# The delta rule's block elimination in other pieces, first retention states on ScalarE, decay exponentials earlier

## The chip, the cores and the metric

One core of a Trainium2 chip runs the whole program in one launch. Its engines each work through a queue of their own, in order: TensorE (PE, matrix products into PSUM), VectorE (DVE), ScalarE (ACT), GpSimd (POOL) and SyncE (SP, which issues DMAs). They wait for each other with semaphores only. The metric is device time in microseconds, the median of several runs.

## The reference

Two network blocks follow each other on 256 tokens of width 1024, in fp32. The first has dilated attention, a gated linear recurrence and two convolutional feed-forward parts. The change lies in the mixer of the second block, which works on 256 context tokens and 256 latent tokens: one projection gives queries, keys and values for four heads of a gated delta rule and four heads of retention, each run forward and backward.

```python
p = (h @ w_in)                         # qkv_a, z, ab, rq, rk, rv, rg
q, k, v = short_conv(qkv_a)            # 5 taps, silu
# gated delta rule, by chunks; G = cumsum of the log decay
decay = exp(G_i - G_j) for i >= j
A = strictly lower part of (beta k k^T * decay)
sol = (A + I)^-1 [beta v, beta k exp(G)]
v_new = u - w S;  o = q_dec S + (q k^T * decay) v_new;  S = g_last S + k_dec^T v_new
o_gdn = rms_norm(o_f + o_b) * silu(z)
# retention, by chunks
o = (q k^T * decay) v + xi (q R);  R = gamma^C R + (k zeta)^T v
o_ret = head_group_norm(r_f + r_b) * silu(rg)
y = concat(o_gdn, o_ret) @ w_out
```

## The kernel before, in words

Tokens are cut in four tiles of 128 (two of context, two latent). Each scan runs over tiles, `TILE_OF` gives the order for the two directions (`DIRS`), and `STEPS` is 4; only steps 2 and 3, the latent tiles, give outputs. fp32 weight products are split: a unit is an eighth of a 2 MB weight chunk or a 128-column strip of it; ACT writes its high part (`high_parts`, L340), DVE subtracts and writes the low part (`low_parts`, L344), and PE multiplies the parts. There are three slots for units (`NPARTS`), so the high part of unit n waits until PE has used unit n-3. The chunks of `w_in` come in the order K, RV, V, RK, Q, Z, RQ, RG, four units each, counted from `u0`: k is 0 to 3, rv 4 to 7, v 8 to 11, rk 12 to 15, q 16 to 19, z 20 to 23, rq 24 to 27, rg 28 to 31. `low_parts(dve, u0 + n)` does all units up to n-1.

The order on every engine is written out by hand, line after line, and is what the change edits.

PE (L2395 to L2511): k, rv, then the v units. Ahead of v's last unit it waits for `EX`, since that unit's bank holds the sums of log decays until ACT has taken their exponential (`EX`, L1373). Then come rk units with log-decay differences and key products between them (`differences`, `key_products`), transposes of v, the units of q, z, rq and rg, transposes of rq and rk, and the retention steps (L2489 to L2511).

ACT (L1365 to L1436): in the loop over v's convolutions i = 4 to 7 it takes a tap (`conv_taps`), a tanh (`conv_tanh`), at i = 5 four copies of turned keys and then `EX`; after the loop the exponentials of the differences (`decay`), then `store_matrix`, which writes the matrices A to DRAM. SP reads their 32x32 diagonal blocks back (L952 to L957) as `blocks`, one block for each partition, and ACT turns the half that belongs to the backward direction (L1395). At the end ACT waits for `inverses`, stores both halves of the inverted blocks to DRAM (L1429, L1432) and loads half of the rows back (L1435); SP loads the other half (L963).

DVE (L1885 to L2043): between the low parts it rotates rk and rq (`rotated`), convolves q (`conv`, `conv_out`), scales z and rg (`gated`) and inverts all blocks at once by elimination (`eliminate`, L1901): for column j it multiplies a column by a row (L1906) and subtracts (L1908), two instructions of up to 240 elements, each waiting for the one before. The columns 1 to 30 stand in six pieces behind low parts. Then the retention steps: update the states (`update_state`, with a plain copy at step 0), mask and multiply the scores (`rPm`), add up outputs (`output_part`). At step 3 DVE expands the inverse rows (`expand`, L1989), from which the delta rule's chain begins: PE's `turn_inverse` (L2537) is its first step.

Of the kernel before, what the change touches and what calls it, by code (L numbers as in the profile page):

```python
# [13 lines left out]
P = 128  # L14
# [101 lines left out]
def build_program(nc, A, out):  # L116
    ctx = ExitStack()
    with ctx:
# [795 lines left out]
        def _(sp):  # L914
# [42 lines left out]
                    sp.dma_start((turned_blocks if d else blocks)[at:at + HB, :, :], source).then_inc(S_("blocks_in"), 16)  # L957
            for i in range(begin_gather, begin_rows):
                load(i)
            sp.wait_ge(S_("inverses_out"), 32)  # L960
            w_rg.done(sp)
            for b in range(NB):
                sp.dma_start(inverse_rows[b * BLK:(b + 1) * BLK, 1, :, :],  # L963
                             block_inverses.ap()[1, b, :, :, :].rearrange("n i j -> i n j")).then_inc(S_("inverse_rows_in"), 16)
            resume = -(-begin_rows // NS)
            for i in range(begin_rows, resume * NS):
                load(i)
# [120 lines left out]
        def _(act):  # L1088
# [276 lines left out]
            for i in range(4, 8):  # L1365
                high_parts(act, u0 + 8 + i)
                conv_taps(i)
                conv_tanh(i)
                if i == 5:
                    for t in range(TT2):  # L1370
                        turned("knT", t)
                    act.wait_ge(S_("sums"), 1)
                    nc_a.activation(EX[:, :, :, :].rearrange("p a b c -> p (a b c)"), ps[:, SUMS_BANK, 0:320], ACT.Exp).then_inc(S_("EX"), 1)  # L1373
            for n in range(4):
                decay(n)
            high_parts(act, u0 + 16)
            for n in (0, 1):
# [46 lines left out]
            for t in LATENT:  # L1424
                turned("rqT", t)

            act.wait_ge(S_("inverses"), 1)
            stored = block_inverses.ap().rearrange("d b n i j -> d (b n) (i j)")
            act.dma_start(stored[0], blocks_flat[0:P // 2, :]).then_inc(S_("inverses_out"), 16)  # L1429
            nc_a.activation(turned_flat[P // 2:P, :], blocks_flat[P // 2:P, ::-1], ACT.Copy).then_inc(S_("blocks_turned"), 1)  # L1430
            act.wait_ge(S_("blocks_turned"), 2)
            act.dma_start(stored[1], turned_flat[P // 2:P, :]).then_inc(S_("inverses_out"), 16)  # L1432
            act.wait_ge(S_("inverses_out"), 32)
            for b in range(NB):
                act.dma_start(inverse_rows[b * BLK:(b + 1) * BLK, 0, :, :],  # L1435
                              block_inverses.ap()[0, b, :, :, :].rearrange("n i j -> i n j")).then_inc(S_("inverse_rows_in"), 16)  # L1436
            def head_squares(kind, t):

                for h in range(H4):
# [106 lines left out]
        def _(dve):  # L1546
# [347 lines left out]
            rotated(w_rk, 0, rk[:, 0, :, :], 0)  # L1894
            low_parts(dve, u0 + 20)
            conv(8)
            rotated(w_rk, 1, rk[:, 1, :, :], 1)
            low_parts(dve, u0 + 21)
            conv_out(8)
            conv(9)  # L1900
            def eliminate(first, end):  # L1901

                for j in range(first, end):
# [7 lines left out]
                    else:  # L1911
                        last.then_inc(S_("inverses"), 1)

            dve.wait_ge(S_("blocks_in"), 16 * 2 * NB)
            dve.wait_ge(S_("blocks_turned"), 1)
            link(v.memset(blocks_flat[:, 0:BLK * BLK:BLK + 1], -1.0))
            eliminate(1, 7)
            low_parts(dve, u0 + 22)
            conv_out(9)
            conv(10)  # L1920
            eliminate(7, 10)
            low_parts(dve, u0 + 23)
            conv_out(10)
            conv(11)
            eliminate(10, 13)
            low_parts(dve, u0 + 24)
            conv_out(11)
            rotated(w_rk, 2, rk[:, 2, :, :], 2)
            low_parts(dve, u0 + 25)
            rotated(w_rk, 3, rk[:, 3, :, :], 3)  # L1930
            eliminate(13, 18)
            low_parts(dve, u0 + 27)
            for i in range(TT):
                gated(w_z, i, zt, TT2)
            eliminate(18, 22)
            low_parts(dve, u0 + 28)
            eliminate(22, BLK - 1)
            for t in LATENT:
                normalized("qn", t)
            low_parts(dve, u0 + 29)  # L1940
            low_parts(dve, u0 + 30)
            low_parts(dve, u0 + 31)
            w_rq.done(dve)
            rotated(w_rq, 0, rq[:, 0, :, :], 0)
            low_parts(dve, u0 + 32)
            rotated(w_rq, 1, rq[:, 1, :, :], TT2 + TT + 1)
            dve.wait_ge(S_("tok_vector"), TT2 + 2 * TT)

            def bc(a):
# [65 lines left out]

            for i in range(TT):
                gated(w_rg, i, rgt, TT2 + TT)
            for d in DIRS:
                dve.wait_ge(S_("decay"), 2 * TT2 + d + 1)
                link(v.tensor_tensor(rET[d], rET[d], bh(cst[:, C_GE if d else C_LE, :]), ALU.mult))  # L2020

            for step in range(STEPS):
                if step >= 2:
                    for d in DIRS:
                        if step > 2:
                            dve.wait_ge(S_("ro"), later(step - 1, d))
                        dve.wait_ge(S_("rqk"), later(step, d))
                        v.tensor_tensor(rPm[d], B4(4 * d), rET[d], ALU.mult).then_inc(S_("rPm"), 1)
                if step < 3:
                    for d in DIRS:  # L2030
                        dve.wait_ge(S_("rdS"), nth(step, d))
                        update_state(rSt[d], 1, step, d, 4 * d + 3, S_("rstate"))
# [155 lines left out]
        def _(pe):  # L2188
# [300 lines left out]
            for step in range(STEPS):  # L2489
                if step >= 2:  # L2490
                    for d in DIRS:
                        t = TILE_OF[d][step]
                        if step > 2:
                            pe.wait_ge(S_("rPm"), later(step - 1, d))
                        heads(4 * d, tile(rkT, t), tile(rqT, t - TT)).then_inc(S_("rqk"), 1)
                    for d in DIRS:
                        t = TILE_OF[d][step]
                        pe.wait_ge(S_("rstate"), nth(step - 1, d))
                        if step > 2:
                            pe.wait_ge(S_("o_out"), later(step - 1, d))  # L2500
                        heads(4 * d + 1, tile(rqT, t - TT), rSt[d])
                if step < 3:
                    for d in DIRS:
                        pe.wait_ge(S_("rkdec"), nth(step, d))
                        if step:
                            pe.wait_ge(S_("rstate"), nth(step - 1, d))
# [276 lines left out]
```

## Time and profile before

| | us |
|---|---|
| median of 3 runs | 1341.31 (1339.39 to 1343.09) |
| span of the profiled execution | 1335.4 |
| PE busy | 1264.9 (95%) |
| DVE busy | 913.2 (68%) |
| ACT busy | 695.0 (52%) |
| POOL busy | 77.0 (6%) |
| PE in the chain that ended last | 78% of the span |

The page gives the span of the profiled execution and no other time of it; the times of the runs are taken apart from it. Engines can be busy at the same time, so the shares don't add up. The mixer of the second block takes the span from about 836 to 1103 us; what the diff touches lies between 896 and 1038 us.

### The profile page before, as it was taken

To read this page: it belongs to the slowest core of one execution; us is meant where nothing else is said; L and a number is where in the kernel's file an instruction comes from. 1 tells how busy PE (TensorE), PEld (TensorE's weight loads), DVE (VectorE), ACT (ScalarE), POOL (GpSimd) and SP (SyncE) were. 2 spreads that over 40 slices of the span, in tenths; PEclk is the share of its full clock that TensorE was granted. 3 is DMA by queue.
4 is the path that set the end of the run, shared out by engine and by line. 5 is a ranking of instruction groups with operands and counts; after the bars stand their busy time and mean duration, and the time that the engine had idled before them with its cause. 6 is when DMAs were issued, how large, how long until landed. Compare 5 with 4: busy or idle time off the path is not lost.

```text
span 1335.4 us, 19244 instructions
## 1 busy us (share of the span) xinstructions
PE 1264.9 (95%) x7760; PEld 1080.7 (81%) x7760; DVE 913.2 (68%) x1429; ACT 695.0 (52%) x1132; POOL 77.0 (6%) x126
## 2 busy tenths in 40 slices
PE   7999999999999999999999999999979889899997
PEld 5899988877888887987888876786758876788885
DVE  4464553447888857687888876755796886766665
ACT  5454544446666645766666755334332444455553
POOL 1000000001000001001000001022011301000000
PEclk9999999999999999999999999999989899899999
DMA  9844335556555557257555557212533006555551
GB/s 336 327 172 145 127 126 190 189 186 241 192 189 192 186 200 265 93 190 291 189 190 189 189 189 266 72 64 103 165 124 101 2 1 212 200 189 191 191 200 48
DMA packets 31718, 230.74 MB, mean 173 GB/s; under 512 B 11000, under 2 KB 14704, under 8 KB 18704
## 3 DMA queue, kind: packets, MB, share of 16 engines
q1 hardware_dynamic: 25568, 218.14, 45.3%
q10 hardware_dynamic: 5056, 7.73, 1.6%
q0 software_dynamic: 1008, 3.67, 0.7%
q8 instruction: 61, 1.00, 0.3%
q14 instruction: 25, 0.20, 0.0%
HBM read 225.82 MB, written 3.71 MB: 172 GB/s over the span
## 4 chain that ended last, share of the span: by engine, by line
PE 78%; DVE 12%; ACT 6%; issue 2%; DMA 1%; POOL 1%; SPq 0%; DVEq 0%; POOLq 0%; ACTq 0%
PE ps L436 18%; PE ps L620 16%; PE ps L499 10%; PE ps L440 9%; PE ps L208 8%; PE ps L488 5%; PE ps L587 4%; DVE parts L344 3%; PE ps L559 3%; PE ps L531 2%; ACT parts L340 2%; DMA ring<-in_W 1%; DVE arena L1655 1%; DVE row L1908 1%; DVE arena L1906 1%
## 5 line engine op out<-in xcount | busy, mean ns | idle before, releaser
L344 DVE TENSOR_TENSOR parts<-ring,parts 128x1024 fp32r<-128x1024 f32 x354 | 431.4, 1224 | 278.5 <-ACT parts L340 201.0
L340 ACT ACTIVATE parts<-ring 128x1024 fp32r<-128x1024 f32 x354 | 372.7, 1057 | 296.6 <-PE ps L440 102.6
L436 PE MATMUL ps<-hall,parts 128*128 128x512 f32 x1120 | 395.1, 398 | 5.5 <-DVE hall L293 3.7
L440 PE MATMUL ps<-hall,parts 128*128 128x256 f32 x1120 | 313.8, 280 | 0.0
L620 PE MATMUL ps<-parts 128*128 128x512 f32 x1128 | 262.0, 391 | 8.6 <-DVE parts L375 8.3
L436 PEld LDWEIGHTS ps<-hall,parts 128*128 128x128 f32 x1120 | 211.1, 188 | 58.4 <-issue 3.3
L620 PEld LDWEIGHTS ps<-parts 128*128 128x128 f32 x1128 | 210.0, 188 | 57.9 <-DVE parts L375 12.6
L440 PEld LDWEIGHTS ps<-hall,parts 128*128 128x128 f32 x1120 | 212.3, 190 | 0.0
L499 PE MATMUL ps<-hall,parts 128*128 128x256 f32 x1152 | 140.7, 284 | 0.0
L499 PEld LDWEIGHTS ps<-hall,parts 128*128 128x128 f32 x1152 | 139.0, 192 | 0.6 <-DVE parts L344 0.5
L208 PE MATMUL ps<-arena 128*128 128x128 f32 (+4 forms) x934 | 111.7, 285 | 16.4 <-DMA arena<-in_onehot 6.5
L208 PEld LDWEIGHTS ps<-arena 128*128 128x128 f32 (+3 forms) x934 | 101.7, 182 | 24.7 <-issue 6.6
L587 PE MATMUL ps<-parts,hall 128*128 128x512 f32 x336 | 85.9, 414 | 8.8 <-DVE parts L344 8.8
L1655 DVE SCALAR_TENSOR_TENSOR arena<-arena,par 128x255 f32<-128x255 f32 (+1 forms) x192 | 80.0, 479 | 18.5 <-ACT arena L1178 17.6
L587 PEld LDWEIGHTS ps<-parts,hall 128*128 128x128 f32 x336 | 66.1, 199 | 25.6 <-DVE parts L344 10.8
L488 PE MATMUL ps<-parts,hall 128*128 128x512 f32 x288 | 69.2, 400 | 1.4 <-DVE hall L297 0.9
L312 POOL TENSOR_SCALAR smallp<-small 128x1 f32<-128x1 f32 x24 | 10.8, 451 | 983.2 <-ACT arena L673 605.7
L488 PEld LDWEIGHTS ps<-parts,hall 128*128 128x128 f32 x288 | 55.2, 193 | 14.6 <-DVE parts L344 3.1
L559 PE MATMUL ps<-hall,parts 128*128 128x512 f32 (+1 forms) x288 | 59.8, 365 | 4.7 <-issue 2.8
L559 PEld LDWEIGHTS ps<-hall,parts 128*128 128x128 f32 x288 | 47.9, 193 | 15.6 <-issue 5.1
L531 PE MATMUL ps<-hall,parts 128*128 128x256 f32 x384 | 48.8, 290 | 1.8 <-DVE hall L297 1.8
L531 PEld LDWEIGHTS ps<-hall,parts 128*128 128x128 f32 x384 | 48.0, 197 | 2.2 <-DVE gates L1576 2.0
(213 smaller groups left out, 1066.0 us busy)
## 6 DMA issues: line engine op xcount, KB each, us to landing
ring<-in_W SPq DMA_DIRECT2D x100, 2048.0 KB, 8.3
arena<-distance_tables SPq DMA_DIRECT2D x8, 384.0 KB, 8.0
gains<-in_gains POOLq DMA_DIRECT2D x5, 512.0 KB, 8.1
ring<-in_W SPq DMA_DIRECT2D x4, 512.0 KB, 9.1
arena<-in_gate_w ACTq DMA_DIRECT2D x1, 2048.0 KB, 10.6
matrices<-arena ACTq DMA_DIRECT2D x8, 256.0 KB, 2.3
x<-in_x SPq DMA_DIRECT2D x2, 512.0 KB, 5.3
gates<-in_ada_gate_b POOLq DMA_DIRECT2D x2, 512.0 KB, 6.3
```

The lines of the kernel that those rows point to most:

```text
L208: return nc.tensor.matmul(o, l, r, start=start, stop=stop)
L340: return nc.scalar.activation(unit_weights(n, 0, weights), weights, ACT.Copy)
L344: return nc.vector.tensor_tensor(unit_weights(n, 1, weights), weights, unit_weights(n, 0, weights), ALU.subtract)
L436: last = nc.tensor.matmul(ps[:, b, :].rearrange("p (a b) -> p a b", a=2), w[:, 0, :], hparts[:, :, k, :], start=k == 0, stop=False)
L440: last = nc.tensor.matmul(ps[:, b, 0:S], w[:, 1, :], hparts[:, 0, k, :], start=False, stop=k == KT - 1)
L488: last = nc.tensor.matmul(ps[:, banks[t], :], hparts[:, x_part, k, t * P:(t + 1) * P], parts[:, u % NPARTS, w_part, w0:w0 + 512], start=k ...
L499: last = nc.tensor.matmul(ps[:, banks[n // 2], (n % 2) * S:(n % 2 + 1) * S], parts[:, u % NPARTS, w_part, k * P:(k + 1) * P], hparts[:, x_ ...
L531: last = nc.tensor.matmul(ps[:, 4 + 2 * (i % 2) + n // 2, (n % 2) * S:(n % 2 + 1) * S], parts[:, u % NPARTS, w_part, k * P:(k + 1) * P], h ...
L559: last = nc.tensor.matmul(o, parts[:, u % NPARTS, w_part, k * P:(k + 1) * P], h, start=k == 0 and x_part == 1, stop=k == KT - 1 and w_part ...
L587: last = nc.tensor.matmul(ps[:, b, :], hall[:, t // TT, x_part, k, t % TT * P:(t % TT + 1) * P], parts[:, u % NPARTS, w_part, w0:w0 + 512] ...
L620: last = nc.tensor.matmul(ps[:, 2 * t + half, :], parts[:, n % NPARTS, x_part, D + t * P:D + (t + 1) * P], parts[:, n % NPARTS, w_part, w0 ...
L1655: last = v.scalar_tensor_tensor(dst, src, pcol("ffn_conv_w", (layer * 3 + tap) * 48 + ft), dst, ALU.mult, ALU.add)
```

## The change: what it does

On ACT `EX` moves ahead of the tanh at i = 5, and the first two decay exponentials ahead of the tanh at i = 7. The copy that turns the backward blocks goes from i = 9 to i = 10, and the high part of unit 23 goes ahead of tanh 11. After the turned queries ACT copies the first retention states (`first_rstate`), and once the inverses are there it turns the backward half and stores it. It then scales the between-tile part of retention's step 2 out of PSUM into the output (`retained`), to which DVE only adds the other part.

On DVE the rotations 0 and 1 of rk come first, then the low parts 19 to 23 with the convolutions of q between them; the elimination starts behind the low part of unit 25 and goes in seven pieces of 3, 2, 2, 3, 2, 4 and 14 columns. The last piece stands behind the gating of rg, directly ahead of the retention steps. The mask of `rET` moves to step 2.

On SP the forward half of the inverses is stored, and all eight loads of rows are issued there, where before ACT issued both stores and four of the loads. PE's waits in the retention follow the new counts.

```diff
 SP
-            sp.wait_ge(S_("inverses_out"), 32)
+            sp.wait_ge(S_("inverses"), 1)
+            sp.dma_start(block_inverses...[0], blocks_flat[0:P // 2, :]).then_inc(S_("inverse_out0"), 16)
             w_rg.done(sp)
-            for b in range(NB):
-                sp.dma_start(inverse_rows[..., 1, :, :], block_inverses.ap()[1, b]...)
+            for d in DIRS:
+                sp.wait_ge(S_(f"inverse_out{d}"), 16)
+                for b in range(NB):
+                    sp.dma_start(inverse_rows[..., d, :, :], block_inverses.ap()[d, b]...)
 ACT
                 conv_taps(i)
+                if i == 5:
+                    act.wait_ge(S_("sums"), 1)
+                    nc_a.activation(EX..., ps[:, SUMS_BANK, 0:320], ACT.Exp).then_inc(S_("EX"), 1)
+                if i == 7:
+                    for n in range(2):
+                        decay(n)
                 conv_tanh(i)
...
-            for n in range(4):
+            for n in range(2, 4):
                 decay(n)
...
-                if i == 9:
+                if i == 10:
                     act.wait_ge(S_("blocks_in"), 16 * 2 * NB)
...
+            high_parts(act, u0 + 24)
             conv_tanh(11)
...
+            for d in DIRS:
+                act.wait_ge(S_("rdS"), nth(0, d))
+                nc_a.activation(rSt[d], B4(4 * d + 3), ACT.Copy).then_inc(S_("first_rstate"), 1)
             act.wait_ge(S_("inverses"), 1)
-            act.dma_start(stored[0], ...)
             nc_a.activation(turned_flat[P // 2:P, :], blocks_flat[P // 2:P, ::-1], ACT.Copy)
-            act.dma_start(stored[1], ...)
-            act.wait_ge(S_("inverses_out"), 32)
-            for b in range(NB): act.dma_start(inverse_rows[..., 0, :, :], ...)
+            act.dma_start(block_inverses...[1], turned_flat[P // 2:P, :]).then_inc(S_("inverse_out1"), 16)
+            for d in DIRS:
+                act.wait_ge(S_("rdS"), nth(2, d))
+                for h in range(H4):
+                    last = nc_a.activation(y2[1][:, t - TT, h, :], ps[:, 4 * d + 1, h * P:(h + 1) * P],
+                                           ACT.Copy, scale=EX[...])
+                last.then_inc(S_("retained"), 1)
 DVE, new order
+            rotated rk 0, rk 1; low_parts(u0 + 20); conv(8)
+            for i in range(8, 12):
+                low_parts(dve, u0 + 13 + i)
+                conv_out(i)
+                if i < 11:
+                    conv(i + 1)
+            rotated rk 2; low_parts(u0 + 25); rotated rk 3; low_parts(u0 + 26)
             dve.wait_ge(S_("blocks_in"), ...); dve.wait_ge(S_("blocks_turned"), 1); memset
+            eliminate(1, 4);   gated z;       low_parts(u0 + 27)
+            eliminate(4, 6);   low_parts(u0 + 28)
+            eliminate(6, 8);   normalized qn; low_parts(u0 + 29)
+            eliminate(8, 11);  low_parts(u0 + 30); rotated rq 0; low_parts(u0 + 31)
+            eliminate(11, 13); low_parts(u0 + 32); rotated rq 1
+            eliminate(13, 17); gated rg
+            eliminate(17, BLK - 1)
 DVE, retention
+                if step == 2 and kind == 1:
+                    dve.wait_ge(S_("retained"), d + 1)
+                    v.tensor_tensor(o_, o_, B4(inner), ALU.add).then_inc(S_("o_out"), 1)
+                    return
...
-                if step < 3:
+                if step in (1, 2):
 PE, retention
-                        pe.wait_ge(S_("rstate"), nth(step - 1, d))
+                        pe.wait_ge(S_("rstate"), nth(step - 2, d))
                         if step > 2:
                             pe.wait_ge(S_("o_out"), later(step - 1, d))
+                            pe.wait_ge(S_("retained"), d + 1)
...
+                        if step == 1:
+                            pe.wait_ge(S_("first_rstate"), d + 1)
```

## Rows read from the trace of the kernel before

**Rows 1.** Page, busy us of each engine (share of span) and instructions.
```profile
PE 1264.9 (95%) x7760; PEld 1080.7 (81%) x7760; DVE 913.2 (68%) x1429; ACT 695.0 (52%) x1132; POOL 77.0 (6%) x126
```
**Rows 2.** Waits of PE, 902 to 1045: us in total, times, longest.
```profile
PE ps L587 <- DVE parts L344: 8.8, 4, 3.2
PE ps L2355 <- DVE arena L1839: 3.1, 1, 3.1
```
**Rows 3.** Chain that ended last, 880 to 1060: start us, us, what.
```profile
896.90 5.54 PE ps L559 x24
902.45 2.85 issue
905.29 7.28 PE ps L559 x24
...
944.93 1.75 PE ps L2355 x16
...
1004.82 10.91 PE ps L587 x48
```
**Rows 4.** Timeline of ACT: start us, us, line, instructions [idle before <- releaser].
```profile
902.83 2.04 ACT L1331 ACTIVATE arena<-ps 128x512 f32<-128x512 f32 x4
904.73 0.46 ACT L1373 ACTIVATE arena<-ps 128x320 f32<-128x320 f32 x1
...
1040.84 1.11 ACT L1462 ACTIVATE arena<-ps 32x128 f32<-32x128 f32 x4 [0.85 <-PE ps L208]
```
**Rows 5.** Stages: us, busy PE, PEld, DVE, ACT, POOL, clock, DMA share, GB/s.
```profile
946.06:1017.65 71.59, 59.62 (x298) 49.66 (x297) 60.18 (x125) 26.73 (x52) 5.56 (x6) 0.88 0.36 115
...
964.32:970.04 5.72, 5.49 (x13) 3.80 (x13) 5.41 (x13) 0.89 (x2) 0.00 (x0) 0.50 0.00 0
...
1000.14:1004.57 4.43, 4.43 (x24) 4.25 (x25) 4.43 (x5) 1.79 (x3) 0.00 (x0) 0.61 0.29 122
...
1018.30:1019.83 1.53, 0.04 (x2) 0.00 (x1) 0.86 (x2) 1.50 (x5) 0.00 (x0) 1.00 0.94 403
...
1022.16:1037.40 15.24, 14.74 (x129) 14.55 (x129) 12.40 (x34) 0.00 (x0) 2.98 (x3) 1.00 0.29 51
```
**Rows 6.** Timeline of PE: z's first unit and the first turn_inverse.
```profile
958.18 2.91 PE L587 MATMUL ps<-parts,hall 128*128 128x512 f32 x12
...
1037.40 1.04 PE L2537 MATMUL ps<-cst,arena 128*128 128x128 f32 x8
```
**Rows 7.** Waits of DVE, 946 to 1037.4: us in total, times, longest.
```profile
DVE parts L344 <- ACT parts L340: 8.4, 3, 4.2
DVE arena L1832 <- ACT arena L1406: 4.6, 1, 4.6
```
**Rows 8.** Stretches, DVE busy of L1906 alone (first three), of L1908 (last).
```profile
946.06:1017.65 71.59, 9.92 (x30) 0.88 0.36 115
959.39:963.04 3.65, 1.56 (x6) 1.00 0.81 346
984.80:1000.00 15.20, 4.55 (x14) 0.89 0.30 101
...
984.80:1000.00 15.20, 4.57 (x14) 0.89 0.30 101
```
**Rows 9.** Timeline of SP's queue: four loads of inverse rows.
```profile
1023.73 2.56 SPq L963 DMA_DIRECT2D arena<-block_inverses x4
```
**Rows 10.** DMA issues, 1015 to 1036: KB each, median us to landing.
```profile
block_inverses<-row ACTq DMA_DIRECT2D x1, 256.0 KB, 4.1
...
arena<-block_inverses SPq DMA_DIRECT2D x4, 64.0 KB, 2.8
```
**Rows 11.** Timeline of DVE in the retention: mask, update of both directions, rPm.
```profile
1017.65 1.54 DVE L2020 TENSOR_TENSOR arena<-arena,cst 128x512 f32<-128x512 f32 x2
...
1023.36 2.16 DVE L1979 SCALAR_TENSOR_TENSOR arena<-arena,ps 128x128 f32<-128x128 f32 x8 [0.75 <-PE ps L208]
1025.43 1.40 DVE L2028 TENSOR_TENSOR arena<-ps,arena 128x512 f32<-128x512 f32 x2
```

More of the change, by code:

```diff
@@ L1367, in _ @@
                 conv_taps(i)
+                if i == 5:
+                    act.wait_ge(S_("sums"), 1)
+                    nc_a.activation(EX[:, :, :, :].rearrange("p a b c -> p (a b c)"), ps[:, SUMS_BANK, 0:320], ACT.Exp).then_inc(S_("EX"), 1)
+                if i == 7:
+                    for n in range(2):
+                        decay(n)
                 conv_tanh(i)
@@ L1371, in _ @@
                         turned("knT", t)
-                    act.wait_ge(S_("sums"), 1)
-                    nc_a.activation(EX[:, :, :, :].rearrange("p a b c -> p (a b c)"), ps[:, SUMS_BANK, 0:320], ACT.Exp).then_inc(S_("EX"), 1)
-            for n in range(4):
+            for n in range(2, 4):
                 decay(n)
@@ L1425, in _ @@
                 turned("rqT", t)
+            for d in DIRS:
+                act.wait_ge(S_("rdS"), nth(0, d))
+                nc_a.activation(rSt[d], B4(4 * d + 3), ACT.Copy).then_inc(S_("first_rstate"), 1)
             act.wait_ge(S_("inverses"), 1)
-            stored = block_inverses.ap().rearrange("d b n i j -> d (b n) (i j)")
-            act.dma_start(stored[0], blocks_flat[0:P // 2, :]).then_inc(S_("inverses_out"), 16)
             nc_a.activation(turned_flat[P // 2:P, :], blocks_flat[P // 2:P, ::-1], ACT.Copy).then_inc(S_("blocks_turned"), 1)
             act.wait_ge(S_("blocks_turned"), 2)
-            act.dma_start(stored[1], turned_flat[P // 2:P, :]).then_inc(S_("inverses_out"), 16)
-            act.wait_ge(S_("inverses_out"), 32)
-            for b in range(NB):
-                act.dma_start(inverse_rows[b * BLK:(b + 1) * BLK, 0, :, :],
-                              block_inverses.ap()[0, b, :, :, :].rearrange("n i j -> i n j")).then_inc(S_("inverse_rows_in"), 16)
+            act.dma_start(block_inverses.ap().rearrange("d b n i j -> d (b n) (i j)")[1],
+                          turned_flat[P // 2:P, :]).then_inc(S_("inverse_out1"), 16)
+            for d in DIRS:
+                t = TILE_OF[d][2]
+                act.wait_ge(S_("rdS"), nth(2, d))
+                for h in range(H4):
+                    last = nc_a.activation(y2[1][:, t - TT, h, :], ps[:, 4 * d + 1, h * P:(h + 1) * P], ACT.Copy,
+                                           scale=EX[:, C_GE if d else C_LE, t, 8 + 4 * d + h:9 + 4 * d + h])
+                last.then_inc(S_("retained"), 1)
             def head_squares(kind, t):
@@ L1893, in _ @@
             w_rk.done(dve)
[L1894 to L1900, printed above, removed]
             def eliminate(first, end):
@@ L1912, in eliminate @@
                         last.then_inc(S_("inverses"), 1)
+            rotated(w_rk, 0, rk[:, 0, :, :], 0)
+            rotated(w_rk, 1, rk[:, 1, :, :], 1)
+            low_parts(dve, u0 + 20)
+            conv(8)
+            for i in range(8, 12):
[3 more added lines that the diff above has]
+                    conv(i + 1)
+            rotated(w_rk, 2, rk[:, 2, :, :], 2)
+            low_parts(dve, u0 + 25)
+            rotated(w_rk, 3, rk[:, 3, :, :], 3)
+            low_parts(dve, u0 + 26)
             dve.wait_ge(S_("blocks_in"), 16 * 2 * NB)
@@ L1916, in _ @@
             link(v.memset(blocks_flat[:, 0:BLK * BLK:BLK + 1], -1.0))
[L1917 to L1932, printed above, removed]
+            eliminate(1, 4)
             for i in range(TT):
                 gated(w_z, i, zt, TT2)
-            eliminate(18, 22)
+            low_parts(dve, u0 + 27)
+            eliminate(4, 6)
             low_parts(dve, u0 + 28)
-            eliminate(22, BLK - 1)
+            eliminate(6, 8)
             for t in LATENT:
@@ L1940, in _ @@
             low_parts(dve, u0 + 29)
+            eliminate(8, 11)
             low_parts(dve, u0 + 30)
-            low_parts(dve, u0 + 31)
             w_rq.done(dve)
             rotated(w_rq, 0, rq[:, 0, :, :], 0)
+            low_parts(dve, u0 + 31)
+            eliminate(11, 13)
             low_parts(dve, u0 + 32)
             rotated(w_rq, 1, rq[:, 1, :, :], TT2 + TT + 1)
+            eliminate(13, 17)
             dve.wait_ge(S_("tok_vector"), TT2 + 2 * TT)
@@ L2017, in _ @@
                 gated(w_rg, i, rgt, TT2 + TT)
-            for d in DIRS:
-                dve.wait_ge(S_("decay"), 2 * TT2 + d + 1)
-                link(v.tensor_tensor(rET[d], rET[d], bh(cst[:, C_GE if d else C_LE, :]), ALU.mult))
+            eliminate(17, BLK - 1)
             for step in range(STEPS):
+                if step == 2:
+                    for d in DIRS:
+                        dve.wait_ge(S_("decay"), 2 * TT2 + d + 1)
+                        link(v.tensor_tensor(rET[d], rET[d], bh(cst[:, C_GE if d else C_LE, :]), ALU.mult))
                 if step >= 2:
@@ L2504, in _ @@
                         pe.wait_ge(S_("rkdec"), nth(step, d))
-                        if step:
-                            pe.wait_ge(S_("rstate"), nth(step - 1, d))
+                        if step == 1:
+                            pe.wait_ge(S_("first_rstate"), d + 1)
+                        elif step:
+                            pe.wait_ge(S_("rstate"), nth(step - 2, d))
                         heads(4 * d + 3, rkdec[d], rv[:, TILE_OF[d][step], :, :]).then_inc(S_("rdS"), 1)
```

7 lines of the change are left out of this document (5 added, 2 removed).

## The prediction, made before the changed kernel was run

> **What bounds the kernel now.** I read the page's busy shares first: TensorE (PE) works in 95% of the span [rows 1], so a gain can only come from the few stretches in which PE waits or runs at half clock. Next I read whom PE waited for between 902 and 1045 us, the stage that the diff touches [rows 2]: 8.8 us in four pieces for low parts that VectorE (DVE) writes, and 3.1 us for the scaled queries (L1839), again DVE. The chain of waits adds a third stop [rows 3]: a piece called "issue", 2.85 us from 902.45. The reader should see that it is no issue at all. PE's program waits there for `EX` ahead of the last v unit, and ScalarE's (ACT's) Exp that signals it runs from 904.73 to 905.19 [rows 4]; PE goes on at 905.29.
>
> Then the stage windows. From 958.18, where the z units begin [rows 6], to the end of rg at 1015.7 PE spends 57.5 us. The twelve units of z, rq and rg at the full-clock price (10.91 us for four, so 2.73 each [rows 3]) are 32.7; sixteen transposes and sixteen decay products between them, at retention's 14.74 us for 128 [rows 5], are about 3.7. So some 21 us are lost: 11.9 in the waits of rows 2, and the rest because PE falls to half clock after them. One z unit took 5.49 us at a granted clock of 0.50; a later stretch had 0.61 [rows 5].
>
> Why is DVE late? From 946.06 to 1017.65 it works almost without a break [rows 5]: its own waits there are 4.2 us for high parts (8.4, less the 4.2 that ends at 946.06) and 4.6 for the rg tanh [rows 7]. The elimination is 30 columns of two instructions, twice 9.9 us busy [rows 8] and about 1.9 of links, 21.8 together, and it stands in pieces in front of the low parts in DVE's one queue: 3.65 us of it ahead of the first z part that PE waits for [rows 8]. In the retention, from 1022.16 to 1037.40, PE is the bound: 14.74 us busy of 15.24 [rows 5].
>
> **The change part by part.** I follow one place: when does PE begin the first `turn_inverse`, at 1037.40 now [rows 6]? All behind it is a chain of small steps among PE, DVE and ACT and then two PE-bound projections; the diff touches none of it, so it moves along rigidly.
>
> *EX ahead of tanh 5.* The Exp needs the sums, ready by 897, and then comes behind tap 5, at about 899. PE reaches its wait at 902.45 and no longer stops: 2.85 us. The v unit behind it took 7.28 us for 24 matmuls against 5.54 for the unit before [rows 3]: 1.74 of half clock, gone too if no stop comes. What is late next: the first rk unit needs the knT copies, done at 904.87 [rows 4], and PE comes at 907.99, so nothing. Of the decay exps 0 and 1 now run ahead of tanh 7; PE wants their banks at about 916, ACT has them by 913.5. So the end of the rk units, 944.93 [rows 3], becomes 940.34, 4.59 earlier. If ACT's order still held PE, this term would be 0.
>
> *DVE's order.* The low part that opens the window of rows 5 starts 1.13 behind the rk units: 941.47. DVE's work from there to the end of both elimination and gated rg is what it is now, 71.59 us less 8.8 of waits, 62.8; only the order differs. Does it wait in the new order? I laid it against PE, instruction by instruction with the durations of the trace. z's four low parts end at 951, 954.5, 958 and 961.5; PE wants them at 953.6, 956.4, 959.1 and 961.8. The fourth rk tile is rotated at 967.0, PE wants it at 965.5: a stop of 1.5. The rq parts come at 965, 968.2, 972.2 and 974.6, wanted at 967, 969.7, 972.5 and 975.2; the rg parts come ahead too. In turn DVE finds each high part ready and waits only some 0.4 us for the rg tanh. PE ends rg near 992 in place of 1015.7, and DVE ends the elimination at 941.47 + 62.8 + 0.4 = 1004.7. PE's 23 us are not the gain: DVE is now the bound, and its last fourteen columns (4.55 + 4.57 busy [rows 8], 10.0 with links) stand in front of retention's second state.
>
> *The block gather* is on SP's queue behind the rq weights, which wait for the last rk unit, so it lands 4.6 earlier too, while ACT's copy of the blocks now comes one tap later. It costs nothing; landing late, it would hold ACT's taps and with them z's low parts, us for us.
>
> *Retention.* ACT's two copies of the first states replace DVE's. A copy of 512 columns is about 0.5 on ACT (four in 2.04 [rows 4]); they lie beside GpSimd's second decayed keys, for which PE waits anyway: nothing, at most 0.2. PE is through two state products and rqk at about 1003.2 and then waits for the state of step 1: 1004.7 plus one direction, half of 2.16 [rows 11], is 1005.8. Six groups of 16 matmuls are left to it; eight took 14.74 [rows 5], so 1.84 each and 11.1: 1016.9. DVE holds them up by 0.3, since 2.16 of update, 1.54 of mask and 1.40 of rPm [rows 11] come first: 1017.2. The `retained` pieces on ACT, 128 columns out of PSUM with a column factor, are not in this trace: between 0.13 each (a quarter of a copy) and 0.5 (a whole one). I take 0.28, the nearest row, four pieces of 128 columns in 1.11 [rows 4], so 1.1 for a direction. They start at the third state product, about 1009, and DVE comes for them at 1012: nothing, and 1 us at the upper end. DVE saves 1.1 us for each direction in step 2, inside PE's six groups: no gain at the end.
>
> *Inverses through DRAM.* SP now stores one half and issues all loads; ACT stores the other. From 1004.7: 4.1 us for the store [rows 10], eight loads on one queue at 2.56 for four [rows 9], so 5.1, and 2.8 to land [rows 10]: 1016.7, and DVE's `expand` needs them. With its 0.64 the transposes start at 1017.4. Now two queues share the loads and the rows arrive 7 us early; then the path is level with PE's. The new waits hold nothing else: behind SP's stands the next weight load, whose chunk is used near 1100; behind ACT's its own share of the retention.
>
> *Clock.* PE stops for some 2.5 us at 1003.2, as it waits for DVE's columns. After the stops of 2.85 and 3.2 us in this trace the next work took 1.74 and 2.76 longer [rows 3, 5]; a stop of 1.5 at 1018.30 cost nothing [rows 5]. I put 1.8 on the path, with ends 0 and 2.8: 1019.2.
>
> **Sum.** 1037.4 - 1019.2 = 18.2 us, so a span of 1335.4 - 18.2 = 1317.2. The page gives no time of the profiled execution beside its span; the median of the runs, 1341.31, is 5.9 above the span, and I carry that over: 1323.1, written as 1323.
>
> **Rivals.**
> *Half clock all through the retention.* For it: granted clock 0.50 from 964 to 970, where PE went at DVE's pace [rows 5]. Against it: in the retention now it is 1.00 in spite of a stop of 1.5 us just ahead [rows 5]. Six groups at twice 1.84 add 11.1 in place of 1.8: a gain of 8.9, 1332.4. The Trainium skill, page "TensorE: Matmul & The Clock Gate", section "What's actually happening", says that the chip halves PE's clock by how busy PE has lately been. By that rule this rival is the regular case wherever PE goes at DVE's pace, and the time would be 1332.4; the trace agrees in the stretches of rows 5 at 0.50 and 0.61, and cannot show it for the new retention.
>
> *The EX wait gives way to another.* PE stops at the knT copies, a difference or a key product instead, and the 4.59 come back: a gain of 13.6, 1327.7. For it: ACT and DVE are only 1 to 3 us ahead of PE there in my layout. Against it: rows 2 name no other engine that PE had to wait for there.
>
> *Slower: the backlog comes back behind the tail.* If z and rq are late because of all of DVE's other work (fourteen low parts, rotations, convolutions) and not of the columns, nothing is won ahead, and 10.0 us of columns follow gated rg: the elimination ends at 1027.7, the transposes start 12.7 + 1.8 later, at 1042.2, 4.8 later than now: 1346. It decides if gated rg ends after 1012.9 (now 1017.65). Against it: the part that PE waits for first has 3.65 us of columns directly in front of it [rows 8], more than the 3.2 that PE waits. That the pieces don't leave the low parts' path is the same case.
>
> **How the numbers follow.** Forecast, 1319 to 1327, 0.62; half clock all through 0.16; EX 0.10; better than 1319 0.04; slower 0.04; a mixture that ends within 4 us of now 0.04. Three thousandths, 4 us, is about what a measurement of this kernel can tell from no change. The time is 1323. The low end, 1317, lies 4 below the same sum without the clock's 1.8, since DVE's short rows may pack better than laid out; the high end, 1333, takes in the half clock. Faster 0.92, same 0.04, slower 0.04.
>
> **What would show it.** After the change: no "issue" piece at 902 in the chain; no wait of PE on L344 above 1 us between 950 and 1000, and a granted clock of 1.00 there; rg ended by 993 to 996; the last columns ended by 1004 to 1007 and PE waiting behind them for the update; `turn_inverse` near 1019. It is wrong if PE's waits on L344 in this stage still sum to 5 us, if DVE stands idle for several us ahead of the last columns, or if `expand` waits long for its rows.

## The result and the profile after

The changed kernel takes 1323.19 us (median of 4 runs, 1321.14 to 1326.27), the kernel before, run beside it, 1340.35 (median of 4, 1334.72 to 1343.09). The ratio is 0.9884 with an interval of 0.9862 to 0.9906: 17.2 us less. The profiled execution has a span of 1319.3 us, 16.1 below that of the kernel before; its own time was 1321.14. Of the runs of the kernel before that stand beside the experiments, one took 1572.18 us at a granted clock of 0.749 and is left out of the median given there.

Absolute times drift by more than 4 us between executions already ahead of the changed stage. So I compare stages from one mark, the piece of the chain with the sums of log decays (ten matmuls of L208; 895.84 before, 895.74 after), to the first `turn_inverse`. I call this the stage length: 141.56 us before, 126.18 after, 15.4 less.

The busy shares, which answer to [rows 1]:

```profile
PE 1256.0 (95%) x7760; PEld 1075.7 (82%) x7760; DVE 915.2 (69%) x1419; ACT 697.8 (53%) x1142; POOL 78.4 (6%) x126
```

PE is busy 8.9 us less with the same 7760 matmuls: that is half clock gone, not work (in the stage the granted clock rose from 0.93 to 0.97). The chain of waits from the mark on (start us, us, what) answers to [rows 3]:

```profile
895.74 1.06 PE ps L208 x10
896.80 10.99 PE ps L559 x48
907.78 2.72 PE ps L587 x12
...
929.23 10.93 PE ps L587 x48
940.18 1.07 ACT parts L340
...
991.53 1.26 DVE row L1917
992.82 1.14 DVE arena L1915
...
1009.67 12.42 PE ps L208 x96
```

The v units are one piece of 10.99 us, where before a stop of 2.85 and a slow unit of 7.28 stood. From 940 to 1009 the chain now runs through DVE: it is the bound of the stage. PE's waits from 896 to 1045 (us in total, times, longest), against [rows 2]:

```profile
PE ps L208 <- DVE arena L1994: 7.3, 1, 7.3
PE ps L208 <- ACT arena L1335: 1.9, 1, 1.9
PE ps L587 <- DVE arena L1844: 1.2, 1, 1.2
```

All waits on L344 are gone. One long one is new, for the state update (L1994) behind the last columns. The stretches (us, busy time of PE, PEld, DVE, ACT, POOL, clock, DMA share, GB/s) answer to [rows 5]:

```profile
958.00:996.00 38.00, 34.89 (x183) 29.42 (x182) 36.62 (x70) 17.92 (x39) 4.80 (x6) 1.00 0.47 168
941.27:1008.49 67.22, 57.55 (x350) 50.58 (x348) 64.49 (x125) 30.02 (x58) 9.25 (x10) 0.98 0.43 139
...
1009.67:1011.69 2.02, 2.02 (x9) 2.02 (x10) 1.99 (x6) 0.00 (x0) 0.00 (x0) 0.50 0.98 229
1011.69:1013.80 2.11, 2.11 (x17) 2.11 (x16) 1.57 (x3) 0.00 (x0) 0.00 (x0) 0.76 0.55 96
1013.80:1021.92 8.12, 8.12 (x75) 8.12 (x74) 7.36 (x17) 2.17 (x8) 0.00 (x0) 1.00 0.32 50
```

The granted clock is 1.00 from 958 to 996, where it fell to 0.50 and 0.61 before. After the wait of 7.28 us it is low for only 4.1 us. But DVE's stretch, from the first low part to the end of the elimination, is 67.2 us long, where the prediction had 63.2 (62.8 of work, 0.4 of a wait). The surplus stands in a few lines of DVE's timeline (start us, us, line, operation, shapes):

```profile
991.53 1.25 DVE L1917 TENSOR_TENSOR row<-row,arena 128x240 f32<-128x240 f32 x1
992.82 1.13 DVE L1915 TENSOR_TENSOR arena<-row 128x240 f32<-128x240 f32 x1
993.98 0.41 DVE L1917 TENSOR_TENSOR row<-row,arena 128x240 f32<-128x240 f32 x1
...
997.38 1.11 DVE L1915 TENSOR_TENSOR arena<-row 128x228 f32<-128x228 f32 x1
998.52 1.12 DVE L1917 TENSOR_TENSOR row<-row,arena 128x228 f32<-128x228 f32 x1
999.67 1.14 DVE L1915 TENSOR_TENSOR arena<-row 128x220 f32<-128x220 f32 x1
1000.85 1.12 DVE L1917 TENSOR_TENSOR row<-row,arena 128x220 f32<-128x220 f32 x1
1002.00 0.38 DVE L1915 TENSOR_TENSOR arena<-row 128x210 f32<-128x210 f32 x1
```

Six instructions of one kind take 1.11 to 1.25 us, their neighbours of the same shape 0.38 to 0.41. GpSimd's timeline shows what ran beside them: retention's decayed keys, in these two stretches and nowhere else in the stage:

```profile
991.48 2.21 POOL L1039 TENSOR_TENSOR arena<-arena 128x512 f32<-128x512 f32 x2 [20.97 <-PE ps L587]
997.02 4.70 POOL L1039 TENSOR_TENSOR arena<-arena 128x512 f32<-128x512 f32 x4 [3.34 <-PE ps L208]
```

In the kernel before, the same keys began at 1015.89, and the last column had ended at 999.5:

```profile
1015.89 2.04 POOL L1035 TENSOR_TENSOR arena<-arena 128x512 f32<-128x512 f32 x2 [28.06 <-PE ps L587]
```

The two never met there. The change brings them together from both sides: PE is through with rg earlier, so the keys start earlier, and the columns end later.

### The profile page after: what moved, and what is told of

Read it like the earlier page. It is cut to its first block, busy times and chain, and to the rows that moved or that the text cites. A ratio compares the mean times of both kernels' runs of the same rounds, so it can differ in the third digit from the quotient of the medians.

```text
span 1319.3 us, 19248 instructions
## 1 busy us (share of the span) xinstructions
PE 1256.0 (95%) x7760; PEld 1075.7 (82%) x7760; DVE 915.2 (69%) x1419; ACT 697.8 (53%) x1142; POOL 78.4 (6%) x126
## 4 chain that ended last, share of the span: by engine, by line
PE 78%; DVE 13%; ACT 6%; issue 2%; DMA 1%; POOL 1%; SPq 0%; DVEq 0%; POOLq 0%; ACTq 0%
PE ps L436 19%; PE ps L620 16%; PE ps L499 10%; PE ps L440 10%; PE ps L208 8%; PE ps L488 5%; DVE parts L344 4%; PE ps L587 3%; PE ps L559 3%; ACT parts L340 2%; PE ps L531 2%; DMA ring<-in_W 1%; DVE row L1917 1%; DVE arena L1915 1%; DVE arena L1671 1%
## 5 line engine op out<-in xcount | busy, mean ns | idle before, releaser
L344 DVE TENSOR_TENSOR parts<-ring,parts 128x1024 fp32r<-128x1024 f32 x354 | 433.0, 1227 | 272.4 <-ACT parts L340 193.2
L436 PEld LDWEIGHTS ps<-hall,parts 128*128 128x128 f32 x1120 | 211.4, 189 | 59.1 <-issue 2.8
L440 PEld LDWEIGHTS ps<-hall,parts 128*128 128x128 f32 x1120 | 212.0, 189 | 0.0
L499 PEld LDWEIGHTS ps<-hall,parts 128*128 128x128 f32 x1152 | 139.0, 192 | 0.6 <-DVE parts L344 0.5
L208 PE MATMUL ps<-arena 128*128 128x128 f32 (+4 forms) x934 | 113.8, 288 | 23.4 <-DVE arena L1994 7.3
L208 PEld LDWEIGHTS ps<-arena 128*128 128x128 f32 (+3 forms) x934 | 103.5, 185 | 31.9 <-DVE arena L1994 7.5
L587 PE MATMUL ps<-parts,hall 128*128 128x512 f32 x336 | 79.0, 393 | 1.2 <-DVE arena L1844 1.2
L587 PEld LDWEIGHTS ps<-parts,hall 128*128 128x128 f32 x336 | 62.6, 188 | 14.8 <-DVE arena L1844 1.5
L488 PE MATMUL ps<-parts,hall 128*128 128x512 f32 x288 | 68.3, 397 | 1.4 <-DVE hall L297 0.9
L488 PEld LDWEIGHTS ps<-parts,hall 128*128 128x128 f32 x288 | 54.6, 191 | 14.3 <-DVE parts L344 3.0
L559 PEld LDWEIGHTS ps<-hall,parts 128*128 128x128 f32 x288 | 48.3, 193 | 10.5 <-issue 1.8
L1182 ACT ACTIVATE arena<-arena,par 128x256 f32<-128x256 f32 x96 | 49.6, 588 | 0.2 <-DVE arena L419 0.2
```

The source lines that it names most:

```text
L208: return nc.tensor.matmul(o, l, r, start=start, stop=stop)
L344: return nc.vector.tensor_tensor(unit_weights(n, 1, weights), weights, unit_weights(n, 0, weights), ALU.subtract)
L436: last = nc.tensor.matmul(ps[:, b, :].rearrange("p (a b) -> p a b", a=2), w[:, 0, :], hparts[:, :, k, :], start=k == 0, stop=False)
L440: last = nc.tensor.matmul(ps[:, b, 0:S], w[:, 1, :], hparts[:, 0, k, :], start=False, stop=k == KT - 1)
L488: last = nc.tensor.matmul(ps[:, banks[t], :], hparts[:, x_part, k, t * P:(t + 1) * P], parts[:, u % NPARTS, w_part, w0:w0 + 512], start=k ...
L499: last = nc.tensor.matmul(ps[:, banks[n // 2], (n % 2) * S:(n % 2 + 1) * S], parts[:, u % NPARTS, w_part, k * P:(k + 1) * P], hparts[:, x_ ...
```

## The experiments

The theory going in: DVE's columns ahead of the low parts had stopped PE, `EX` was a stop of its own, and both are gone; DVE is now the bound, lengthened by GpSimd's keys. The first four ran together, with 1339.20 for the kernel before (median of 15), then the other four, with 1338.35 (median of 7).

**`EX` back in its old place, all else as changed.**

```diff
-                if i == 5:          # ahead of conv_tanh(i)
-                    act.wait_ge(S_("sums"), 1)
-                    nc_a.activation(EX..., ACT.Exp).then_inc(S_("EX"), 1)
                 conv_tanh(i)
                 if i == 5:
                     for t in range(TT2):
                         turned("knT", t)
+                    act.wait_ge(S_("sums"), 1)
+                    nc_a.activation(EX..., ACT.Exp).then_inc(S_("EX"), 1)
```

> The changed kernel with one edit undone: the exponential that signals EX stands again behind the four copies of turned keys, after the tanh of i = 5. Theory (each edit pays by its own stop): PE stops for 2.85 us ahead of the last v unit and does 24 matmuls at partly half clock, 7.3 in place of 5.5; the rk units end 4.6 us later, VectorE's long stretch of work starts 4.6 later, and all behind it moves with it: first turn_inverse 4.6 later than 1021.9, time 4.6 above the changed kernel (range 3.5 to 5.5). Rival (VectorE is the bound from before that place and absorbs the stop): turn_inverse and time move by less than 1.5 us.

Measured: 1328.32 us (1325.07 to 1330.24, 5 runs), ratio to the kernel before 0.9924 (0.9899 to 0.995). The stage is 129.86 us long, 3.7 more than in the changed kernel. Its chain:

```profile
896.98 5.54 PE ps L559 x24
902.53 2.87 issue
905.39 5.73 PE ps L559 x24
```

The stop is back at its full size. The unit behind it took 5.73 us, 0.2 over its neighbour, where it took 1.74 over in the kernel before. At the end of the rk units 3.2 of the 3.7 us are there already; the rest came behind them. So `EX` is a stop of its own, as the theory had it, and what varies is the half clock after it.

**Decayed keys on ScalarE instead of GpSimd.**

```diff
 POOL
-            for step in range(STEPS - 1):
-                for d in DIRS: ... decayed_keys(1, step, d, rkdec, rk, S_("rkdec"))
 ACT, around the first_rstate copies
+            def retention_keys(step, d):
+                for h in range(H4):
+                    last = nc_a.activation(rkdec[d][:, h, :], rk[:, t, h, :], ACT.Copy, scale=EX[...])
+                last.then_inc(S_("rkdec"), 1)
```

> The changed kernel with retention's decayed keys (three steps, two directions) on ScalarE, four scaled copies of 128 columns each, in place of GpSimd's six multiplications. In the changed kernel six instructions of the elimination took 1.11 to 1.25 us where their like took 0.39 to 0.42, all six beside those multiplications. Theory (VectorE and GpSimd slow each other while both read two tensors of SBUF): no elimination instruction above 0.45 us, the last column ends 4.4 us earlier (1004.1), PE's wait for the update shrinks from 7.3 to about 3, first turn_inverse at 1017 to 1018 and time 4 to 5 us below the changed kernel. Rival (the six long instructions are VectorE's own, for instance a wait or a PSUM or DMA collision at that time): they stay long, and the time is unchanged or up to 2 us worse, as ScalarE takes 1.1 us for a direction where GpSimd took 1.04.

Measured: 1317.91 us (1317.69 to 1318.33, 5 runs), ratio 0.9845 (0.982 to 0.9871); stage 120.42, 5.8 shorter than the changed kernel's. The groups of DVE's instructions in the two lines of the elimination (count, busy us, mean ns, idle before), first of the changed kernel, then of this one:

```profile
L1917 DVE TENSOR_TENSOR row<-row,arena 128x30 f32<-128x30 f32 (+14 forms) x30 | 12.3, 409 | 1.0
L1915 DVE TENSOR_TENSOR arena<-row 128x30 f32<-128x30 f32 (+14 forms) x30 | 12.1, 404 | 0.8
```

```profile
L1924 DVE TENSOR_TENSOR row<-row,arena 128x30 f32<-128x30 f32 (+14 forms) x30 | 10.0, 333 | 1.0
L1922 DVE TENSOR_TENSOR arena<-row 128x30 f32<-128x30 f32 (+14 forms) x30 | 9.9, 330 | 0.8
```

24.4 us fall to 19.9, what the kernel before spent on them, and the last column ends 4.5 us earlier after the mark. PE's timeline shows the rest:

```profile
999.25 3.64 PE L208 MATMUL ps<-arena 128*128 128x128 f32 x16 [2.72 <-ACT arena L1433]
...
1004.79 14.09 PE L208 MATMUL ps<-arena 128*128 128x128 f32 x120 [0.49 <-ACT arena L1433]
1018.71 1.04 PE L2566 MATMUL ps<-cst,arena 128*128 128x128 f32 x8
```

PE no longer stops for the update, only for ACT's keys: three waits, the longest 2.72 us. From the last column's end (1006.58) to `turn_inverse` it takes 12.1 us in place of 13.4, with the granted clock at 1.00 from 1004.79 on. So 4.5 of the 5.8 us are the columns' own, and 1.3 are won behind them, where PE neither stops nor runs at half clock. This is the lowest median measured, below both kernels.

**Columns back ahead of z's low parts.**

```diff
             for i in range(8, 12):
+                if i == 9: (waits for the blocks, memset)
+                if i > 8:
+                    eliminate(*{9: (1, 7), 10: (7, 10), 11: (10, 13)}[i])
                 low_parts(dve, u0 + 13 + i)
...
-            eliminate(1, 4)      and (4, 6), (6, 8), (8, 11), (11, 13) further down
```

> The changed kernel with the first twelve columns of the elimination moved back ahead of z's second, third and fourth low parts (6, 3 and 3 columns); the columns 13 to 30 stay where the change put them. VectorE does the same work in another order. Theory (columns ahead of low parts make PE stop, and VectorE then has to wait for PE): PE waits for low parts come back, three of 1.5 to 3 us, with granted clocks of 0.5 to 0.8 behind them; rg ends at about 1000 in place of 991, the elimination at about 1016 in place of 1008.5, time 8 us above the changed kernel (range 5 to 11). Rival (the backlog is all of VectorE's other work, the place of the columns is of no account): time within 2 us of the changed kernel.

Measured: 1330.75 us (1327.43 to 1333.9, 10 runs), ratio 0.9937 (0.9921 to 0.9953); stage 133.42, 7.2 longer than the changed kernel's. PE's waits and its fourth z unit:

```profile
PE ps L587 <- DVE parts L344: 7.3, 3, 2.9
PE ps L208 <- DVE arena L1992: 5.6, 1, 5.6
```

```profile
974.03 5.49 PE L587 MATMUL ps<-parts,hall 128*128 128x512 f32 x12 [2.90 <-DVE parts L344]
```

Twelve columns in the old place bring back the waits and a unit at half clock (5.49 us, the length it had in [rows 5]). DVE pays too: it waits 8.6 us longer for high parts, since PE frees their slots later. That is how the columns' place moves the end of the elimination, 7.3 us later after the mark, though the work is the same. What the theory said came, and the rival's 2 us did not, but for the clock: it fell behind the third stop alone (0.50), and was 1.00 in the units behind the other two. The 7.2 us are a net figure: the keys meet narrower columns here, and the two lines of the elimination take 22.9 us instead of 24.4.

**The kernel before with columns 1 to 29 left out.**

```diff
-                for j in range(first, end):
+                for j in range(max(first, BLK - 2), end):
```

> The kernel before with the elimination's columns 1 to 29 left out (column 30 stays, to signal), so the inverses are not computed; everything else in its order. Theory (the columns are what made z, rq and rg late): PE has no wait above 1 us for a low part between 950 and 1000, granted clock 1.00 there, rg ends near 997 in place of 1015.6, and the time falls by 18 to 20 us. Rival (VectorE's other work is enough to hold PE up): waits for low parts of 5 us or more stay, and the time falls by less than 8 us.

Measured, in one run: 1328.91 us, 10.3 below the kernel before; stage 126.53, 15.0 shorter (the profiled execution reached the mark 4.2 us later than that of the kernel before, so the two differ). Its waits of PE:

```profile
PE ps L559 <- issue: 2.9, 1, 2.9
PE ps L587 <- DVE parts L344: 2.3, 2, 1.9
PE ps L587 <- DVE arena L1828: 1.6, 1, 1.6
```

This lies between the theory's figure and the rival's. The columns are most of it, but 3.9 us of stops stay though 29 of the 30 columns are gone (the granted clock behind them is 1.00, as the theory had it). DVE's rotations and convolutions also stood ahead of low parts, and the reorder moves those as well; that they cause these stops was not tested by itself. The unit after the `EX` stop took 8.58 us here. By the stage length the changed kernel, with all its columns, is as quick as the old order without them, which still has the `EX` stop.

**Decayed keys on GpSimd with a factor for each partition, one tensor read in place of two.**

```diff
-                    decayed_keys(1, step, d, rkdec, rk, S_("rkdec"))
+                    for h in range(H4):
+                        last = nc.gpsimd.tensor_scalar(rkdec[d][:, h, :], rk[:, t, h, :], EX[...], None, ALU.mult)
+                    last.then_inc(S_("rkdec"), 1)
```

> The changed kernel with retention's decayed keys still on GpSimd, but as four multiplications of 128 columns by a column factor (one tensor of SBUF read, not two). With these keys off GpSimd no elimination instruction was above 0.41 us, so GpSimd is the other party; open is whether it matters what GpSimd reads. Theory (two two-tensor readers collide): no elimination instruction above 0.45, the last column 4.4 us earlier than in the changed kernel, counted from the sums of log decays (112.7 there), turn_inverse 3 to 5 earlier. Rival (any GpSimd multiplication beside VectorE's two-tensor instructions collides): elimination instructions of 1 us and more stay beside the keys, as many or more of them, as four instructions take GpSimd longer, and time is unchanged to 3 us worse.

Measured: 1319.05 us (1318.2 to 1323.76, 4 runs), ratio 0.9864 (0.9838 to 0.9889); stage 122.97, 3.2 shorter than the changed kernel's. DVE's two lines, and two of their instructions:

```profile
L1919 DVE TENSOR_TENSOR arena<-row 128x30 f32<-128x30 f32 (+14 forms) x30 | 11.2, 374 | 0.8
L1921 DVE TENSOR_TENSOR row<-row,arena 128x30 f32<-128x30 f32 (+14 forms) x30 | 11.2, 374 | 1.0
```

```profile
999.54 0.54 DVE L1921 TENSOR_TENSOR row<-row,arena 128x220 f32<-128x220 f32 x1
1000.12 0.54 DVE L1919 TENSOR_TENSOR arena<-row 128x210 f32<-128x210 f32 x1
```

GpSimd's 24 instructions of 128 elements took 636 ns each, 14.8 us in all, where six of 512 took 1122 ns each, 6.7 in all. The collision is not gone but has another form: DVE's instruction beside them lasts 0.54 us instead of 1.12, over about twice the time. So the last column ends 1.9 us earlier after the mark, less than half of the 4.5 (22.4 us busy). PE's wait for the update falls to 0.81, but it now waits twice for GpSimd's slower keys, 2.7 us in all; its six groups behind the last column then run at a granted clock of 1.00 and take 10.96 us instead of 12.25, the other 1.3 of the 3.2 us. The instructions held to neither expectation, the 0.45 of the theory or the 1 us of the rival. The run changes length and form of GpSimd's instructions at once, so it can't say which of the two sets the 0.54.

**The `retained` pieces back on VectorE.**

```diff
-            for d in DIRS: ... nc_a.activation(y2[1]..., ACT.Copy, scale=EX[...]) ... S_("retained")
-                if step == 2 and kind == 1:
-                    dve.wait_ge(S_("retained"), d + 1)
-                    v.tensor_tensor(o_, o_, B4(inner), ALU.add).then_inc(S_("o_out"), 1)
-                    return
-                            pe.wait_ge(S_("retained"), d + 1)
```

> The changed kernel with the output of retention's step 2 formed on VectorE again, a copy and four scaled adds for a direction in place of one add; ScalarE's eight scaled copies are gone. Theory 1 (as in the prediction, VectorE's saving lies inside PE's six groups and is worth nothing at the end): turn_inverse and time within 0.7 us of the changed kernel. Theory 2 (in the trace after, VectorE is busy from the last column to the rPm of step 3 with less than 1.5 us of waits, so 2.3 us more on it hold up rPm and with it PE's last groups): 1 to 2.5 us later.

Measured: 1323.3 us (1322.05 to 1325.04, 4 runs) beside 1323.13 for the changed kernel on the same chip; stage 126.84 against 126.29. PE waits 0.51 us for DVE ahead of the last 24 matmuls. By the stage the move is worth half a microsecond, by the medians nothing that can be told.

**The first retention states back on VectorE.**

```diff
-            for d in DIRS: ... nc_a.activation(rSt[d], B4(4 * d + 3), ACT.Copy) ... S_("first_rstate")
-                if step in (1, 2):
+                if step < 3:
... (and the waits of PE and DVE that name `first_rstate`)
```

> The changed kernel with the first retention states copied by VectorE again, in its place behind the last column; PE's second state product waits for it. Theory (the columns at the tail are only affordable since ScalarE lets PE do two groups ahead of the wait): PE waits longer for VectorE and does the second state product after the columns, VectorE adds 1.4 us of copies and then waits for PE: turn_inverse and time 3 us later (2 to 4.5). Rival (PE's groups are short enough to be made up behind the wait): less than 1 us later.

Measured: 1327.45 us (1324.98 to 1328.47, 4 runs), 4.3 above the changed kernel; stage 129.13, 2.8 longer. PE's wait and DVE's instruction that ends it:

```profile
PE ps L208 <- DVE arena L1988: 8.7, 1, 8.7
```

```profile
1009.06 1.28 DVE L1988 COPY arena<-ps 128x512 f32<-128x512 f32 x2
```

On DVE even the first state stands behind the last columns, so PE stops one round earlier, with eight groups still to do instead of six. The copies themselves are the smaller part of what the move to ACT is worth. Here too the figure is net: with PE stopped, two of the keys miss the columns, and the elimination takes 23.1 us in its two lines instead of 24.4.

**The changed kernel again, beside the last three.**

> The changed kernel itself, on the same chip as the three runs beside it, as their yardstick: stage from the sums of log decays to the first turn_inverse 126 us, time about 1323, PE's wait for the update about 7 us, six elimination instructions above 1 us beside GpSimd's keys. Theory: all of it repeats. Rival: the six long instructions were an accident of one execution.

Measured: 1323.13 us (1320.9 to 1326.4, 4 runs), ratio 0.9891 (0.9869 to 0.9912); stage 126.29; the same six slow instructions, 24.4 us in the two lines. What is read from the profile above repeats.

## Why the prediction was right, and what in it was not

The time was predicted as 1323 and came out as 1323.19. The mechanism was right, but some terms were mis-sized, and errors of opposite sign met in the sum.

- **`EX`: right.** The stop and the slow unit are gone, nothing took their place, and the first low part starts at 941.27 (predicted 941.47). ACT's Exp ran at 898.37. Of the 4.59 us only the 2.85 of the stop is firm: the half clock after the same stop was worth 0.2, 1.74 and 3.0 us in three executions.
- **DVE's order, PE's side: right.** No wait on L344, clock 1.00, one stop of 1.2 us for the fourth rk tile (predicted 1.5), rg ended at 991.3 (predicted near 992). The gather of the blocks held nothing up: DVE began on them at 967.63 without a wait.
- **DVE's order, the elimination: the step that failed.** It ended at 1008.49, not 1004.7. The 62.8 us of work took the columns' durations from a stretch without GpSimd's keys [rows 8]. The changed order puts GpSimd's keys beside them, and 19.9 us become 24.4. That the collision is the cause is shown: without the keys on GpSimd the durations are the old ones, and with other keys they are others. None of the rows that I used shows such a cost, and a GpSimd engine at 6% of the span [rows 1] looked harmless. But the trace of the kernel before has it, just ahead of the stage: a low part of 1.45 us, where most take 1.22, beside two GpSimd multiplications that took 3.02, where the two shown above took 2.04:

```profile
891.25 3.02 POOL L1028 TENSOR_TENSOR gains<-cst,arena 128x512 f32<-128x512 f32 x2
891.92 1.45 DVE L344 TENSOR_TENSOR parts<-ring,parts 128x1024 fp32r<-128x1024 f32 x1
```

- **Retention: right in form.** PE waits behind the last columns for the update, 7.28 us instead of 2.5, and six groups follow. They took 12.25 us, where 11.1 + 0.3 + 1.8 had been put: the clock cost 1.2, and the longer stop did not cost more. Half clock all through, the first rival, did not come: the clock was low for 4.1 us, and 1.00 after. The other two rivals did not come either: no wait took the place of `EX`, and gated rg ended at 995.7, far ahead of the 1012.9 that was to decide.
- **Inverses through DRAM: mis-sized, without effect.** The rows' path was put level with PE's. It was shorter. Queue and landing times of the changed kernel:

```profile
1011.65 4.05 SPq L967 DMA_DIRECT2D arena<-block_inverses x8
```

```profile
arena<-block_inverses SPq DMA_DIRECT2D x8, 64.0 KB, 2.2
block_inverses<-row SPq DMA_DIRECT2D x1, 256.0 KB, 3.0
```

  That is 3.0, 4.05 and 2.2 us in place of 4.1, 5.1 and 2.8. The rows are there near 1017.9, before `expand` starts at 1019.23. With the 12.0 us of the prediction behind the late elimination they would have come at 1020.5 and held it up.
- **`retained` on ACT: right in size.** 0.27 us for a piece (0.28 taken). At the end it was put at nothing; by the stage of the run without it, it is worth half a microsecond.

At the first `turn_inverse` this makes 3.9 us late from the elimination and 1.1 early behind it: it stands at 1021.92, 2.8 after the place that was predicted (the mark is 0.1 earlier). The stage won 15.4 us and not 18.2. What follows it was 0.6 us shorter, so the span fell by 16.1.

The rest of the agreement is luck. The span came out at 1319.3 where 1317.2 had been put, 2.1 too long; the median lies 3.9 above that span where 5.9 had been carried over, 2.0 too little, and the two errors cancel. Every run here has a time about 1.8 us above its own span, so the profiled execution of before, with 1335.4, was a quick one, some 4 us under the median known then, and the 5.9 held those 4 as well. The profiled execution after lies only 2.0 under its median. Measured by medians the gain is 17.2, with a median of before that fell by 1.0 with its fourth run.

By the experiments the parts of the 15.4 us are: place of the first twelve columns 7.2, `EX` 3.7, first states on ACT 2.8, `retained` about 0.5. The 1.2 that are left were not taken apart (each figure is what undoing one part alone costs, net of what it changes in the meeting with GpSimd's keys, so they need not add up; the split store of the inverses, the exponentials ahead of tanh 7, and the order of rotations and convolutions belong to them).

## What to carry to other kernels

When work is moved on one engine, look at what will then run beside it on the others, GpSimd above all: durations from the old neighbourhood hold only there. In one queue, put the long work with a late reader behind the short work with an early reader; what it wins is the waits and the half clock after them, and a part comes back where the long work ends. Compare stages from a mark inside the same execution, since a span carries several microseconds of drift from elsewhere.

## What the runs showed of the hardware

DVE's products and differences of two SBUF tensors, 220 to 240 elements wide, take 0.38 to 0.41 us alone and 1.11 to 1.25 us beside GpSimd's multiplication of two tensors of 512 elements (1.12 us each). In the stretch from 997.02 exactly four of DVE's lie beside four of GpSimd's. The Trainium skill, page "GPSIMD Engine Reference", section "Specifications", says that GpSimd shares its SBUF interfaces with VectorE and contends with VectorE's instructions that have two SBUF inputs. These rows agree, and put the price at a factor of nearly three. DVE's low parts met the same in the changed kernel: two of them took 1.94 and 1.85 us beside GpSimd's multiplications near 912 and 923, where most take 1.22.

The clock's price after a stop is not a function of the stop alone: three stops of 2.85 to 2.87 us at the same place cost 0.2, 1.74 and 3.0 us, and one of 7.28 us elsewhere 1.2. The granted clock in the 24 matmuls behind the three was 1.00, 0.77 and 0.64 (`EX` back, the kernel before, and the one without columns; columns as in [rows 5]):

```profile
905.39:911.12 5.73, 5.72 (x25) 4.75 (x26) 4.13 (x5) 2.01 (x3) 0.00 (x0) 1.00 0.73 237
905.29:912.57 7.28, 7.28 (x25) 5.92 (x26) 4.82 (x6) 2.06 (x3) 0.00 (x0) 0.77 0.74 263
909.53:918.12 8.59, 8.59 (x25) 6.83 (x26) 4.82 (x6) 2.05 (x3) 0.00 (x0) 0.64 0.67 246
```
